# Two transformer blocks on one core: wide matrix products as plain fp32 instead of three f32r matmuls

## What is computed

```python
def first_block(x, ...):
    h = rmsnorm(x, norm1_g)
    p = h @ w_in                      # 1024 -> 1920 rwkv, 1536 q/k/v, 2048 gates
    p_rwkv, q, k, v, gate_logits = split(p)
    y_a = rwkv7_bidirectional(p_rwkv, ...) @ w_o_rwkv      # 512 -> 1024
    y_b = neighbourhood_attention_2d(q, k, v, ...) @ w_o_na
    g_a, g_b = split(sigmoid(gate_logits + b_gate))
    x = x + (g_a * y_a + g_b * y_b) @ w_out                # 1024 -> 1024
    return x + hierarchical_moe(rmsnorm(x, norm2_g), ...)  # 32 experts

def second_block(x, c, ctx, c_ctx, ...):
    sh1, sc1, g1, sh2, sc2, g2 = split(silu(c) @ w_mod + b_mod)
    h, hc = modulate(x, norm1_g, sh1, sc1), modulate(ctx, norm1_g, csh1, csc1)
    z, zc = h @ w_in, hc @ w_in       # Hyena, GLA and gated-delta-net heads
    x = x + g1 * (concat(hyena, gla, gdn) @ w_out)
    h = modulate(x, norm2_g, sh2, sc2)
    x = x + g2 * (square(relu(h @ w1)) @ w2)               # 1024 -> 4096 -> 1024
    return rmsnorm(x, final_norm_g)
```

## Time and profile before

| | us |
|---|---|
| median of 3 runs | 2109.08 |
| lowest, highest | 2106.25, 2110.61 |
| span of the profiled execution (first to last instruction) | 2095.9 |
| PE busy in it | 1930.3 |
| DVE busy | 1017.8 |
| ACT busy | 633.9 |
| POOL busy | 264.8 |

### The profile page before, as it was taken

One profiled execution on the slowest core, in us unless ns is written; L12 is line 12 of the kernel. 1 busy time (PEld: TensorE's weight loads), 2 busy tenths in 40 slices (PEclk: granted clock), 3 DMA queues, 4 the chain that ended last, 5 costly groups with the idle time before them and its releaser, 6 DMA issues. The chain is left out here.

```text
span 2095.9 us, 42448 instructions
## 1 busy us (share of the span) xinstructions
PE 1930.3 (92%) x18014; PEld 1432.8 (68%) x18014; DVE 1017.8 (49%) x1836; ACT 633.9 (30%) x1172; POOL 264.8 (13%) x459
## 2 busy tenths in 40 slices
PE   6999999999999869877899998999998899999997
PEld 4776678787748733222678775477787777888886
DVE  6666544434278721110458655465665673333333
ACT  4555432332132212211337331112211333322321
POOL 1000152342100011111000000012322001100100
PEclk9999999999999879999799999999999999999998
DMA  5222100000057899999722102320001242322331
GB/s 197 83 80 66 46 26 13 23 13 13 23 193 243 305 358 410 409 409 405 279 99 64 57 21 90 138 71 23 23 3 63 92 131 81 99 92 91 100 100 41
DMA packets 73985, 265.82 MB, mean 127 GB/s; under 512 B 10966, under 2 KB 11478, under 8 KB 72784
## 3 DMA queue, kind: packets, MB, share of 16 engines
q1 hardware_dynamic: 60848, 225.69, 29.5%
q10 hardware_dynamic: 7488, 25.95, 3.5%
q0 software_dynamic: 5472, 11.59, 1.5%
HBM read 254.57 MB, written 17.30 MB: 130 GB/s over the span
## 5 line engine op out<-in xcount | busy, mean ns | idle before, releaser
L216 DVE TENSOR_TENSOR weights_lo<-ring,weights_hi 128x1024 fp32r<-128x1024 f32 x140 | 173.3, 1239 | 146.1 <-ACT weights_hi L212 146.1
L212 ACT CAST weights_hi<-ring 128x1024 fp32r<-128x1024 f32 x140 | 146.1, 1045 | 258.2 <-PE ps L242 254.5
L241 PE MATMUL ps<-wide_b_round,weights_hi 128*128 128x512 f32 (+1 forms) x384 | 141.2, 368 | 0.0
L240 PE MATMUL ps<-wide_b_round,weights_hi 128*128 128x512 f32 (+1 forms) x360 | 131.1, 364 | 2.1 <-DVE wide_a_round L3949 2.1
L242 PE MATMUL ps<-wide_b_round,weights_lo 128*128 128x512 f32 (+1 forms) x360 | 130.3, 362 | 0.0
L240 PE MATMUL ps<-mlp_hi,weights_hi 128*128 128x512 f32 x320 | 125.7, 393 | 4.1 <-DVE mlp_lo L3899 4.1
L241 PE MATMUL ps<-mlp_lo,weights_hi 128*128 128x512 f32 x320 | 125.0, 391 | 0.0
L242 PE MATMUL ps<-mlp_hi,weights_lo 128*128 128x512 f32 x320 | 125.0, 391 | 0.0
L241 PE MATMUL ps<-wide_a_round,weights_hi 128*128 128x512 f32 x256 | 101.2, 395 | 0.0
L240 PE MATMUL ps<-wide_a_round,weights_hi 128*128 128x512 f32 x216 | 92.9, 430 | 3.7 <-DVE wide_b_round L663 3.7
L991 PE MATMUL ps<-wide_a,ring 128*128 128x256 f32 x320 | 87.6, 398 | 0.7 <-issue 0.7
(11 more groups left out here) (625 smaller groups left out, 4057.5 us busy)
## 6 DMA issues: line engine op xcount, KB each, us to landing
ring<-stream_in SPq DMA_DIRECT2D x210, 512.0 KB, 3.5
moe_ring<-stream_in SPq DMA_DIRECT2D x112, 512.0 KB, 13.4
w_mod<-w_mod_in ACTq DMA_DIRECT2D x40, 512.0 KB, 6.5
wide_b<-stream_in SPq DMA_DIRECT2D x32, 512.0 KB
xT<-w_mod_in SPq DMA_DIRECT2D x16, 512.0 KB, 4.3
na_rel<-rel_in POOLq DMA_DIRECT2D x4, 640.0 KB, 6.2
mod_acc<-mod_part ACTq DMA_DIRECT2D x5, 512.0 KB, 6.2
ring<-mod_acc SPq DMA_DIRECT2D x1, 2560.0 KB, 18.5
```

The costliest lines, as they stand in the source:

```text
L212: act.copy(self.hi[:, i % self.n, :], w).then_inc(self.cast.sem, self.cast.up())
L216: ins = eng.tensor_tensor(self.lo[:, i % self.n, :], self.unit(i)[0], self.hi[:, i % self.n, :], ALU.subtract)
L240: pe.matmul(out, left[0], right[0], start=start, stop=False, **kw)
L241: pe.matmul(out, left[0], right[1], start=False, stop=False, **kw)
```

## The change

All products through `Split` become one plain fp32 matmul each, with the weights read from the ring itself. `Split`, `product`, `rounded` and the type F32R go. `Core.unit` takes a ring unit and waits for its landing; the last matmul of a unit raises `k.used`, which now frees the ring slot and tells ACT and DVE that the result is there. The moving sides are single fp32 tiles: `k.A` in heads and core (the joins go), `yaT`, `ybT` and the gates in merge, `mix_h` in mixer_in, `k.B` in the tail's MLP. For the context, `hc` is one fp32 view of `k.B`. Since h is one tile, it is stored to a new device tensor `h_mid` once its eighth block is ready, before SP streams units 6 and on of mixer_in; in hyena one transfer of 2 MB brings it back into ring slots 0 to 3, issued behind win and ahead of the wait for `both_done`. In the tail the MLP is no longer halved: 32 units of the first layer, then 8 times 4 units of the second; ACT takes relu into a tile `mlp_hidden` of 32 blocks, DVE squares in place, POOL does nothing there. The order of the MLP units in the stream changes with it. The filler matmuls and their numbers stay, but in the tail both head transposes now follow kt 1 of the first out2 unit.

```diff
+    def unit(self, pe):
+        w, landed, full = self.take()
+        pe.wait_ge(landed, full)
+        return w
...
-class Split:
...
-def product(pe, out, left, right, start, stop, **kw):
...
 # stage_heads, PE
-                    w.ready(pe, u)
+                    w = k.unit(pe)
...
-                                pe.wait_ge(h_rested.sem, h_rested.at(kt + 1))
-                            mm = product(pe, k.ps[:, u % 3, :], w.parts(u, kt * P, (kt + 1) * P), (h[0][:, kt, :], h[1][:, kt, :]),
-                                         kt == 0, kt == DB - 1)
+                                pe.wait_ge(h_scaled.sem, h_scaled.at(kt + 1))
+                            mm = pe.matmul(k.ps[:, u % 3, :], w[:, kt * P:(kt + 1) * P], h[:, kt, :], start=kt == 0, stop=kt == DB - 1)
                         if half:
-                            mm.then_inc(w.done.sem, w.done.up())
+                            mm.then_inc(k.used, 1)
...
 # stage_core, PE and DVE
-                        if u == 0 and at == 0:
-                            pe.wait_ge(h_joined.sem, h_joined.at(kt + 1))
...
-                for b in range(5):
-                    join(b)
...
 # stage_merge, PE, out units
-                            pe.wait_ge(rested.sem, rested.at(kt + 1))
-                        mm = product(pe, k.ps[:, i, :], w.parts(8 + i, kt * P, (kt + 1) * P), mix_parts(kt), kt == 0, kt == DB - 1)
-                        if kt == 0:
-                            mm.then_inc(k.used, 1)
-                    mm.then_inc(w.done.sem, w.done.up())
+                            pe.wait_ge(m_done.sem, m_done.at(max(6, kt + 1)))
+                        mm = pe.matmul(k.ps[:, i, :], w[:, kt * P:(kt + 1) * P], gate(kt), start=kt == 0, stop=kt == DB - 1)
+                    mm.then_inc(k.used, 1)
...
 # stage_mixer_in, PE and SP
+                            wk = w[:, kt * P:(kt + 1) * P]
+                            mm = pe.matmul(lat(u), wk, h[:, kt, :], start=kt == 0, stop=kt == DB - 1)
                             if kind in WITH_CTX:
+                                mm = pe.matmul(ctx(u), wk, hc[:, kt, :], start=kt == 0, stop=kt == DB - 1)
...
                 sp.dma_start(k.dram["x_mid"], k.xT[:, :, :]).then_inc(saved.sem, saved.up(16))
+                sp.wait_ge(h_ready.sem, h_ready.at(DB))
+                sp.dma_start(k.dram["h_mid"], h[:, :, :]).then_inc(h_saved.sem, h_saved.up(16))
                 k.stream(sp, N, 0)
...
 # stage_hyena, SP
                 sp.dma_start(win, k.dram["hy_win"]).then_inc(tap_in.sem, tap_in.up(16))
+                sp.dma_start(k.ring[:, 0:4, :], k.dram["h_mid"].rearrange("p (i a) t -> p i (a t)", a=2)).then_inc(h_back.sem, h_back.up(16))
                 sp.wait_ge(both_done.sem, both_done.at(4 * NT))
...
 # stage_tail
-    HB = 16
-    U2 = 2 * DB
-    N = DB + 2 * (HB + U2)
+    HB = 32
+    PER = HB // DB
+    N = DB + 2 * HB
...
+                        if (i, kt) == (0, 2):
+                            turn_heads(0)
+                            keep_busy(k, pe, 6, 7)
+                            turn_heads(1)
+                            keep_busy(k, pe, 4, 7)
+                        if i == 0 and kt >= 2:
+                            pe.wait_ge(hn_gated.sem, hn_gated.at(kt - 1))
...
+                for i in range(HB):
+                    act.wait_ge(k.used, k.after(DB + i))
+                    act.activation(hid[:, i, :], k.ps[:, i % 8, :], ACT.Relu).then_inc(relu_done.sem, relu_done.up())
...
+                for i in range(HB):
+                    dve.wait_ge(relu_done.sem, relu_done.at(i + 1))
+                    dve.tensor_tensor(hid[:, i, :], hid[:, i, :], hid[:, i, :], ALU.mult).then_inc(hid_done.sem, hid_done.up())
```

More of the change, by code:

```diff
@@ L190, in block @@
         return self.nc.Block()
-class Split:
[L196 to L235, removed]
-def product(pe, out, left, right, start, stop, **kw):
-    pe.matmul(out, left[0], right[0], start=start, stop=False, **kw)
-    pe.matmul(out, left[0], right[1], start=False, stop=False, **kw)
-    return pe.matmul(out, left[1], right[0], start=False, stop=stop, **kw)
 def keep_busy(k, pe, n, bank):
@@ L504, in leave @@
                     ps = k.ps[:, u % 3, :]
-                    w.wait(act, u)
+                    act.wait_ge(k.used, k.after(u))
                     if kind == "r":
@@ L685, in _ @@
                 for u in range(len(units)):
-                    if u + 2 < len(units):
-                        w.rest(dve, u + 2)
                     if u and units[u - 1][0] == "r":
@@ L1383, in _ @@
                         middle(t)
-                    if t == 0:
-                        for b in range(5, DB):
-                            join(b)
                     for lv in range(1, FAST):
@@ L1537, in _ @@
                 for i in range(8):
-                    w.ready(pe, i)
+                    w = k.unit(pe)
                     if i < 2:
@@ L1724, in _ @@
                 for i in range(8):
-                    w.rest(dve, 2 + i)
-                    w.wait(dve, i)
+                    dve.wait_ge(k.used, k.after(LATE + i))
                     for j in range(2):
@@ L1985, in stage_moe @@
             assert k.taken == first and k.issued == first + MOE_RING == first + U
-            ctx_in, c_scaled, c_rounded, c_rested, c_chain, c_done = (
-                k.sig("ctx_" + x) for x in ("landed", "scaled", "rounded", "rested", "chain", "done"))
+            ctx_in, c_scaled, c_ready, c_chain = (k.sig("ctx_" + x) for x in ("landed", "scaled", "ready", "chain"))
             assert all(s.base == 0 for n, s in k.signals.items() if n.startswith(("own_", "dense_")))
@@ L2195, in context @@
                 def context():
-                    counts = [(x, x.n) for x in (norm.squared, norm.rooted, m_copied, c_rounded)]
+                    counts = [(x, x.n) for x in (norm.squared, norm.rooted, m_copied, c_ready)]
                     act.wait_ge(ctx_in.sem, ctx_in.at(16))
@@ L2558, in leave @@
                     kind, b = units[i]
-                    w.wait(act, i)
+                    act.wait_ge(k.used, k.after(i))
                     if kind in CONV:
@@ L2682, in leave @@
                         return
-                    w.wait(dve, i)
+                    dve.wait_ge(k.used, k.after(i))
                     if kind == "gv":
@@ new lines, in _ @@
+                for i in range(HB):
+                    w = k.unit(pe)
+                    if i == 6:
+                        pe.wait_ge(m_added.sem, m_added.at(1))
+                    if i >= 8:
+                        pe.wait_ge(relu_done.sem, relu_done.at(i - 7))
+                    for kt in range(DB):
+                        if i == 0:
+                            pe.wait_ge(h_ready.sem, h_ready.at(kt + 1))
+                        mm = pe.matmul(k.ps[:, i % 8, :], w[:, kt * P:(kt + 1) * P], h[:, kt, :], start=kt == 0, stop=kt == DB - 1)
+                    mm.then_inc(k.used, 1)
@@ new lines, in _ @@
+                for i in range(DB):
+                    pe.wait_ge(relu_done.sem, relu_done.at(HB - 7 + i))
+                    for j in range(PER):
+                        w = k.unit(pe)
+                        for kt in range(8):
+                            f = 8 * j + kt
+                            if i == 0:
+                                pe.wait_ge(hid_done.sem, hid_done.at(f + 1))
+                            mm = pe.matmul(k.ps[:, i, :], w[:, kt * P:(kt + 1) * P], hid[:, f, :], start=f == 0, stop=f == HB - 1)
+                        mm.then_inc(k.used, 1)
@@ L3880, in _ @@
+                for i in range(HB):
+                    act.wait_ge(k.used, k.after(DB + i))
+                    act.activation(hid[:, i, :], k.ps[:, i % 8, :], ACT.Relu).then_inc(relu_done.sem, relu_done.up())
+                for b in range(DB):
+                    act.wait_ge(x_done.sem, x_done.at(DB + b + 1))
+                    last.square(act, b, k.xT[:, b, :])
+                last.root(act)
             @block.vector
@@ new lines, in _ @@
+                for i in range(HB):
+                    dve.wait_ge(relu_done.sem, relu_done.at(i + 1))
+                    dve.tensor_tensor(hid[:, i, :], hid[:, i, :], hid[:, i, :], ALU.mult).then_inc(hid_done.sem, hid_done.up())
+                for b in range(DB):
+                    dve.wait_ge(k.used, k.after(DB + HB + PER * b + PER - 1))
+                    dve.scalar_tensor_tensor(k.xT[:, b, :], k.ps[:, b, :], mlp_factor(b), k.xT[:, b, :], ALU.mult, ALU.add).then_inc(x_done.sem, x_done.up())
+                    if b > 1:
+                        last.add(dve, b - 1)
```

316 lines of the change are left out of this document (48 added, 268 removed).

## The result

The changed kernel takes 2266.07 us (median of 4 runs, 2260.11 to 2272.37), the kernel before 2108.65 (2106.25 to 2110.61). The ratio is 1.0761, 95% interval 1.0710 to 1.0811: slower by 7.6%. 2270 was predicted, in a range of 2250 to 2296. The profiled execution of the changed kernel has a span of 2260.0 us where the one before had 2095.9: 164.1 more, where the sum said 161.0.

A forecast was written before the change was run, and what follows sets the result against it. PE (TensorE), busy 92%, was taken to bound every stage the change touches. The 2109.1 us median plus 195.4 for dearer products, less 34.4 regained from PE's waits, gave 2270.1, taken as 2270; range 2250 to 2296.

The forecast's parts named there:

- The price of a product: All 512-column products on PE: 0.858 us as plain fp32 against 0.68 to 0.70 for three f32r matmuls; +187.3 us.
- rival 3: All products: a plain fp32 matmul costs one record, 0.429 us, so the kernel gets faster, about 1800 us; chance 0.04.
- rival 4: All products: four streams at f32r's spacing, 0.92 us a product in place of 0.858, 2337 us; chance 0.01.
- Rival 1: Unit starts and merge: PE waits for scaling, attention chain or w_mod instead, so nothing comes back; 2304 us; chance 0.09.
- rival 5: All products: the compiler does not really make them otherwise, so the time stays at 2109 us; chance 0.01.
- What came back: Stage starts, merge, attention and joins: time regained where PE had waited for rounding; -34.4 us in all.
- Heads, unit 0: First unit of heads: PE starts right behind the filler and ends at 31.7, only scaling ahead of it; -6.7 us.
- MLP, unit 0: First MLP unit, paced before by two DVE steps per block: ends 6.86 us behind the filler; -4.0 us.
- out2, unit 0: First out2 unit in the tail: done near 1671.4 instead of 1676.9, behind filler and head transposes; -6.9 us.
- In merge: Merge's out units: without the weights' rests on DVE, PE leads; 5 of 6 us come back, some w_mod wait may stay.
- The transfers of h: Mixer and hyena: 2 MB to h_mid and 2 MB back are covered by other work; 0 us, +16 if neither were.
- The step that failed: Weight ring: slots released 5 to 7 us later are covered by six slots and 6.9 us units; no cost.

The follow-up runs named there:

- b_four: Kernel before with four f32r matmuls for a product, the low parts' product added to the three; 2361.51 us, ratio 1.1215.
- b_tail_plain: Kernel before with only the tail stage (out2, MLP) and its weight order from the changed kernel, as plain fp32; 2192.44 us, ratio 1.0401.
- a_h_twice: Changed kernel with the mixer input written to device memory twice and read back twice; 2271.90 us, ratio 1.0777.
- a_early: Changed kernel with SP's small loads (w_up, a_up, two rows) moved ahead of the last four ring units of heads; 2263.78 us, ratio 1.0743.
- a_early_busy: Changed kernel with SP's small loads early, plus eight filler matmuls in each of the last two levels of core's last inverse; 2263.79 us, ratio 1.0773.
- b_two: Kernel before with two f32r matmuls for a product, weights' high part times input's low part left out, all roundings kept; 1939.64 us, ratio 0.9196.
- b_one: Kernel before with one f32r matmul for a product, both low-part terms and the weights' rests left out; 1792.93 us, ratio 0.8534.

## Why the prediction was right

**The price of a product** held. 0.858 us was worked out from line 1523's records and came out at 0.858 in the MLP, with the stages of heads, mixer and tail within 1.4 us of the sum; rival 3 (one record a product, 1800 us) and rival 4 (0.92, 2337 us) are excluded by the 512 records of 0.429. b_four has four matmuls at rival 4's spacing, with the roundings kept, and took 2361.51. Rival 1 (2304) would have shown in the stages below, and rival 5 (2109) in the time.

**What came back** held to a few us. Heads, unit 0: the first product starts at 24.45 and unit 1 near 31.3, where 31.7 stood. MLP, unit 0, and out2, unit 0, in the changed kernel:

```profile
1730.73 8.33 PE L195 MATMUL ps<-const 128*128 128x128 f32 x60 [2.44 <-PEq L2914]
...
1745.47 7.03 PE L3599 MATMUL ps<-wide_a,ring 128*128 128x512 f32 x16
...
1750.89 0.75 DVE L3703 SCALAR_TENSOR_TENSOR xT<-ps,mod,xT 128x512 f32<-128x512 f32 x1 [3.98 <-PE ps L3599]
...
1804.23 2.17 PE L195 MATMUL ps<-const 128*128 128x128 f32 x18
...
L3658 ACT ACTIVATE mlp_hidden<-ps x32: 597/597/598, 1813.3 to 2026.2; 128x512 f32<-128x512 f32 x32
```

out2's unit 0 is done 11.8 us behind the filler's end (11.8 expected, 17.3 before), the MLP's 6.9 (6.9 expected, 9.5 before). From the first relu to the last addition it is 432.6 us, against the 432 expected. Two terms were a little small. In merge the sum took back 5 of the 6 us by which the stage exceeded PE's work; PE is now busy for 72.9 of 73 us there, so that all came back, which is some 1 of the 2.7 us; the other part is not placed. Nor were the 6 us all DVE's lag, as the prediction read them: from 716.4 to 719.4 us lines 240 to 242 start 0.43 us apart where they otherwise start 0.23 apart, at the lower clock level, which is some 1.4 us. And the stage of the experts ended 2.7 us sooner, relative to its start, than before, for which the sum had nothing. 1.7 of them lie at the end of merge: from its last addition to the routing stage's first matmul it is 5.9 us before and 4.2 after (5.9 in b_tail_plain, whose merge is the one before). Before, PE's logits (line 1514) wait 2.0 us for that addition and the next step (line 1572) takes 1.87 us; after, it takes 1.05 (line 1465).

**The transfers of h** are free, as said. The way back takes 14.9 us and not 8.2, in traffic, but a_h_twice shows that not even the double matters.

**The step that failed** is this one: "A ring slot is released by the product's end and no longer by the rest, 5 to 7 us later; with six slots and units of 6.9 us that is covered". For the units it is true. But a wait on a queue holds whatever stands behind it, and the prediction had not asked what that was on SP at the end of heads: four small loads on which the stage ends. 8.8 us, by a_early. The sum came out near all the same (161.0 for 164.1), because merge and the experts gave back 5.4 more than was claimed. That two misses of opposite sign met is luck.

**From span to median** the prediction kept 13.2 us. It was 6.1 this time. The gap says how the profiled execution stands among the others. Both profiled executions were without the long low stretch in core (327.7 us from first gate product to merge before, 327.5 after), and over the four runs of the changed kernel the clock falls as the time grows (0.973, 0.970, 0.965 and 0.966 at 2260.11, 2261.83, 2270.31 and 2272.37 us). That the low stretches make up the gap in the runs without a trace is argued, not shown. The prediction lies 4.0 above the median: 3.1 too few in the span, 7.1 too many here. This too is luck in part.

## What to carry to other kernels

Count a matmul's records against the loop that issues it before you price it: one plain fp32 instruction here is two records and 0.858 us, and so loses to three f32r matmuls (0.69), while it wins against four (0.93). When a release moves later, ask not only whether the transfer it frees is still early enough, but what stands behind the wait on the same queue, at the ends of stages above all. And a matmul taken off each product of a full PE is worth less each time, as the chains behind it come to light: 255 us for the fourth, 167 for the third (some 220 with the weights' rests gone too) and 88 for the second, the last two in kernels that leave terms out. So look at the shortest unit that the other engines can deliver before you promise it.

## What the runs showed of the hardware

- 128x512 from start to start: 0.233 to 0.235 us for an f32r matmul in the MLP of b_four, 0.858 for a plain fp32 one (two records 0.429 apart), which is 3.7 of them.
- A wait of 5.8 us in place of 0.8 was followed by instructions of 1.6 to 1.9 times the length, at a granted clock of 0.52; with the wait gone they were normal, at 1.00. The wait's price was 8.8 us.
- A busy PE does not keep the high clock for certain: in a_early_busy PE is busy for 15.91 of 16 us from 540 to 556 us at 1.00, and then for 15.00 of 15.00 from 560 to 575 at 0.52. In the traces with such a stretch the core stage takes 336.6 to 338.6 us, and 327.5 in the one without.
- The mean granted clock is lower in the kernels in which PE has less to do: 0.970 in the changed kernel (PE busy 94% of the span), 0.941 in b_two (88%), 0.903 in b_one (83%).
